# A delta net of chunk steps: the preparation, the doubling and the scan in one loop over the chunks

## What is computed

```python
decay = exp(where(incl, Gcum[..., :, None] - Gcum[..., None, :], -inf))
A = where(strict, einsum('bhnid,bhnjd->bhnij', k * beta, k) * decay, 0.0)
t_inv = triangular_solve(A + eye, eye, lower=True, unit_diagonal=True)
W = t_inv @ (k * beta * exp(Gcum))
U = t_inv @ (v * beta)
attn = einsum('bhnid,bhnjd->bhnij', q, k) * decay
def step(S, xs):
    v_new = U_n - W_n @ S
    o = q_n * exp(Gcum) @ S + attn_n @ v_new
    S = S * exp(G_total) + k_tail_n.T @ v_new
```

## Time and profile before

| what | value |
| --- | --- |
| median of 3 runs | 2021.78 us (2018.9 to 2022.38) |
| profiled execution, its own time | 2022.69 us |
| its span in the trace | 2020.9 us |
| granted PE clock, mean | 0.961 of full |
| delta net, from the phase end before it to the first branch matmul | 267.1 to 517.7 us of the span |

### The profile page before, as it was taken

The page is one execution under the profiler, slowest core; times in us unless marked ns, Lnnn a source line. Parts: engine busy times, 40 slices in busy tenths (PEclk is TensorE's granted clock), DMA queues, the critical chain, the costliest instruction groups (busy, mean ns, idle before and its releaser), DMA issues.

```text
span 2020.9 us, 34275 instructions
## 1 busy us (share of the span) xinstructions
PE 1845.8 (91%) x11766; PEld 1644.9 (81%) x11766; DVE 1273.1 (63%) x2464; ACT 1014.5 (50%) x2022; POOL 154.1 (8%) x116
## 2 busy tenths in 40 slices
PE   7999978778789997689999999999999997989997
PEld 1877867778678997678899999999899886879997
DVE  1684347777425997966666666666676665236776
ACT  2445533333015667866655555555557655016655
POOL 0000003221015452000000000000000000000000
PEclk9899978889889999999999999999999998999999
DMA  7423202222234552035555555555454432444553
GB/s 266 174 102 105 84 11 94 81 81 70 90 108 167 177 177 73 1 104 194 195 183 187 186 187 186 187 187 187 156 178 148 157 116 92 137 145 157 183 181 124
DMA packets 77266, 283.72 MB, mean 140 GB/s; under 512 B 8576, under 2 KB 8576, under 8 KB 76800
## 3 DMA queue, kind: packets, MB, share of 16 engines
q1 hardware_dynamic: 77184, 282.62, 40.9%
HBM read 281.54 MB, written 1.05 MB: 140 GB/s over the span
## 4 chain that ended last, share of the span: by engine, by line
PE 69%; DVE 13%; ACT 3%; issue 1%; POOL 1%; POOLq 0%; DVEq 0%; ACTq 0%
PE banks L702 17%; PE banks L690 16%; PE banks L764 8%; PE banks L897 6%; PE banks L654 6%; PE banks L909 3%; PE banks L575 2%; DVE split L1791 2%; PE banks L589 1%; PE banks L869 1%; DVE arena L1789 1%; DVE arena L1629 1%; DVE arena L1592 1%; PE banks L778 1%; PE banks L641 1%
## 5 line engine op out<-in xcount | busy, mean ns | idle before, releaser
L1130 ACT ACTIVATE split<-arena 128x512 fp32r<-128x512 f32 x508 | 319.1, 629 | 146.7 <-PE banks L690 83.2
L690 PEld LDWEIGHTS banks<-split 128*128 128x128 f32 x3072 | 379.5, 192 | 12.8 <-POOL split L2146 3.4
L690 PE MATMUL banks<-split 128*128 128x256 f32 x3072 | 383.0, 283 | 4.8 <-POOL split L2146 2.3
L702 PE MATMUL banks<-split 128*128 128x512 f32 x1536 | 365.0, 392 | 2.7 <-issue 2.7
L1805 DVE TENSOR_TENSOR split<-arena,split 128x512 fp32r<-128x512 f32 x412 | 281.6, 690 | 117.0 <-ACT split L1130 111.3
L702 PEld LDWEIGHTS banks<-split 128*128 128x128 f32 x1536 | 284.5, 189 | 58.8 <-issue 2.9
L1120 ACT ACTIVATE split<-arena 128x512 fp32r<-128x512 f32 x264 | 163.6, 626 | 73.2 <-PE banks L764 29.8
L764 PE MATMUL banks<-split 128*128 128x256 f32 x1344 | 169.3, 286 | 4.0 <-DVE split L1887 3.9
L764 PEld LDWEIGHTS banks<-split 128*128 128x128 f32 x1344 | 164.6, 193 | 7.6 <-issue 5.9
L424 PE MATMUL banks<-split 128*128 128x256 f32 (+2 forms) x936 | 152.3, 325 | 8.2 <-DVE split L1451 7.2
L424 PEld LDWEIGHTS banks<-split 128*128 128x128 f32 (+1 forms) x936 | 135.6, 198 | 26.9 <-issue 8.8
(11 more groups left out here) (365 smaller groups left out, 2398.9 us busy)
## 6 DMA issues: line engine op xcount, KB each, us to landing
arena<-wstream SPq DMA_DIRECT2D x525, 512.0 KB, 3.2
arena<-x_t SPq DMA_DIRECT2D x1, 2048.0 KB, 12.3
arena<-matsa SPq DMA_DIRECT2D x1, 1234.0 KB, 6.4
arena<-mats SPq DMA_DIRECT2D x1, 1024.0 KB, 9.3
out_t<-arena SPq DMA_DIRECT2D x4, 256.0 KB, 2.1
arena<-crow SPq DMA_DIRECT2D x1, 512.0 KB, 7.2
arena<-rows SPq DMA_DIRECT2D x1, 512.0 KB, 3.9
arena<-mats SPq DMA_DIRECT2D x1, 449.0 KB, 3.9
```

What stands on the lines that cost most here:

```text
L690: mm = pe.matmul(ps[:, 4 + b, 0:S], w_parts[:, c, (2 * m + half) % 4, P * k:P * k + P], h_parts[:, e, 4 * half + k, :], start=(half == 0 a ...
L702: mm = pe.matmul(ps[:, 2 * tt + half, :], g_parts[:, e, j % 2, P * tt:P * tt + P], w_parts[:, c, (2 * m + half) % 4, :], start=(first and ...
L1130: act.activation(w_parts[:, 0, (2 * m + half) % 4, :], ring[:, peer_slot(m), 512 * half:512 * half + 512], ACT.Copy).then_inc(sem["w_hi"], 1)
```

## The change

The three pieces become one loop of four steps.

- The small decay functions move into the attention phase; sigmoid is made from an exponential and a reciprocal, and a dummy exponential loads the table before the stage. One phase end is dropped.
- Within a level, PE multiplies the unmasked A with only those 64 columns a head of Z that the level changes (`parts`), VectorE masks the product (`packed`, 128x256) while it takes it out of PSUM, and the update has 64 columns too. ScalarE moves only the turned Z. Level 1 also turns Z, since T isn't made apart any more. Six of the seven masks and GpSimd's mask products go.
- While step n goes through its levels, the next chunk is prepared at fixed levels: rows of decays at 1, gaps and key products at 2, decayed keys, betas and the first mask on VectorE (`decayed_keys`, `mask_keys`) at 3, query products at 4, the turn of the mask at 5, the first Z at 6. Key products are now made for each direction apart, since the backward direction takes its own chunk order (`scan`).
- The scan of step n - 1 runs inside step n, and tokens are turned in levels 1 to 4 of step 0. GpSimd scales keys, values and states instead of masking.
- One tail stands at each level's end instead of one behind each Z, two in four of the levels; four more stand ahead of the loop. Silu and sigmoids of gates move to step 3.
- In the attention phase half of the attention output is turned earlier, and spread roots use three banks.

The core of the diff: PE's levels and loop, VectorE's helpers and loop, GpSimd's loop.

```diff
+            def level_products(n, l, d):
+                z, a = pair[d][f"Z{n % 2}"], pair[d][f"A{n % 2}"]
+                if l == 1:
+                    pe.wait_ge(sem["z1_ready"], step_at(n, d))
+                else:
+                    pe.wait_ge(sem["z_ready"], level_at(n, l - 1, d))
+                for h in range(4):
+                    mm = pe.matmul(ps[:, d, 64 * h:64 * h + 64], a[:, h, :], parts(z[:, h, :], l, 1 - d), start=True, stop=True)
+                mm.then_inc(sem["y_done"], 1)
...
+                    mm = pe.transpose(ps[:, 2 + d, P * h:P * h + P], z[:, h, :], ident)
+                mm.then_inc(sem["z_turned"], 1)
+
+            def level_update(n, l, d):
+                if l < 6:
+                    pe.wait_ge(sem["y_out"], 10 * n + 2 * (l - 1) + d + 1)
+                else:
+                    pe.wait_ge(sem["y_last"], step_at(n, d))
+                pe.wait_ge(sem["t_ready"], level_at(n, l, d))
+                r = slice(0, P) if l < 6 else slice(64 * d, 64 * d + 64)
+                for h in range(4):
+                    mm = pe.matmul(ps[:, d, 256 + 64 * h:320 + 64 * h], pair[d]["T"][r, h, :], yp[d][r, 64 * h:64 * h + 64],
+                                   start=True, stop=True)
+                mm.then_inc(sem["p_done"], 1)
+
...
+            for n in range(4):
+                for l in range(1, 7):
+                    for d in range(2):
+                        level_products(n, l, d)
+                    if n == 0 and l < 5:
+                        tok_turn(2 * l - 2)
+                        tok_turn(2 * l - 1)
+                    for d in range(2):
+                        if n and l == 1:
+                            state_write(0, d) if n == 1 else state_read(n - 1, d)
+                        if n == 3 and l == 2:
+                            query_read(2, d)
+                        if n >= 2 and l == 3:
+                            state_write(n - 1, d)
+                        if n == 3 and l == 4:
+                            out_write(2, d)
+                        if n == 3 and l == 5:
+                            query_read(3, d)
+                        if 1 <= n < 3 and l == 4:
+                            query_products(n + 1, d)
+                    for d in range(2):
+                        level_update(n, l, d)
+                    if n < 3:
+                        for d in range(2):
+                            if l == 1:
+                                decay_rows(n + 1, d)
+                            if l == 2:
+                                key_products(n + 1, d)
+                            if l == 5:
+                                mask_turn(n + 1, d)
                 for d in range(2):
-                    pe.wait_ge(sem["gb_ready"], 2 * n + d + 1)
-                    for h in range(4):
...
+            def gap_rows(n, d):
+                dve.wait_ge(sem["g_rows"], step_at(n, d))
+                e = pair[d]["E"]
+                gap = e if n < 2 else at[:, 2 * d + scan[d][n], :, :]
+                link(dve.tensor_tensor(gap, bank(4 + d, 4, P), head("G", n, d), ALU.subtract))
+                o = dve.tensor_scalar(e, gap, 0.0, None, ALU.max)
+                if n >= 2:
+                    link(o)
+                    o = dve.tensor_scalar(gap, gap, 0.0, None, ALU.min)
+                o.then_inc(sem["gaps"], 1)
+
+            def decayed_keys(n, d):
+                dve.wait_ge(sem["decays"], step_at(n, d))
+                dve.wait_ge(sem["k_products"], step_at(n, d))
+                dve.tensor_tensor(pair[d][f"A{n % 2}"], pair[d]["E"], bank(4 + d if n else 6 + d, 4, P), ALU.mult).then_inc(sem["a_raw"], 1)
+
+            def mask_keys(n, d):
+                b = pair[d]
+                a = b[f"A{n % 2}"]
+                dve.wait_ge(sem["a_raw"], step_at(n, d))
+                link(dve.tensor_tensor(a, a, head("beta", n, d), ALU.mult))
+                dve.tensor_tensor(b["E"], a, bc(level[:, d, :], 1, 4), ALU.mult).then_inc(sem["mask_ready"], 1)
+
+            def decayed_queries(n, d):
+                s = at[:, 2 * d + scan[d][n], :, :]
+                dve.wait_ge(sem["q_products"], step_at(n - 2, d))
+                dve.tensor_tensor(s, s, bank(4 + d, 4, P), ALU.mult).then_inc(sem["at_raw"], 1)
+
+            def first_inverse(n, d):
+                dve.wait_ge(sem["m_turned"], step_at(n, d))
+                dve.tensor_tensor(pair[d][f"Z{n % 2}"], bc(ident, 1, 4), bank(4 + d, 4, P), ALU.subtract).then_inc(sem["z1_ready"], 1)
+
...
+            for n in range(4):
                 for l in range(1, 7):
                     for d in range(2):
...
+                            dve.wait_ge(sem["y_done"], level_at(n, l, d))
+                            dve.tensor_tensor(yp[d].rearrange("p (a b) -> p a b", a=4), ps[:, d, 0:256].rearrange("p (a b) -> p a b", a=4),
+                                              bc(packed[:, d, l - 1, :], 1, 4), ALU.mult).then_inc(sem["y_out"], 1)
+                        elif n < 3:
+                            first_inverse(n + 1, d)
+                    for d in range(2):
+                        dve.wait_ge(sem["p_done"], level_at(n, l, d))
+                        z = parts(pair[d][f"Z{n % 2}"].rearrange("p a b -> p (a b)"), l, 1 - d)
+                        dve.tensor_tensor(z, z, ps[:, d, 256:512].rearrange("p (g s) -> p g s", s=2 ** l), ALU.subtract).then_inc(sem["z_ready"], 1)
+                    for d in range(2):
+                        if n == 1 and l == 1:
+                            new_state(0, d)
+                        if n >= 2 and l == 1:
+                            new_values(n - 1, d)
+                        if n == 3 and l == 2:
+                            query_scale(2, d)
+                        if n < 3 and l == 2:
+                            gap_rows(n + 1, d)
+                        if n < 3 and l == 3:
+                            decayed_keys(n + 1, d)
+                        if n >= 2 and l == 3:
+                            new_state(n - 1, d)
+                        if 1 <= n < 3 and l == 4:
+                            decayed_queries(n + 1, d)
+                        if n == 3 and l == 4:
+                            out_add(2, d)
+                        if n == 3 and l == 5:
+                            query_scale(3, d)
+                    for d in range(2):
+                        if n < 3 and l == 3:
+                            mask_keys(n + 1, d)
+                    for q in range(2 if (n, l) in ((0, 1), (0, 2), (3, 4), (3, 5)) else 1):
+                        mod_tail(next(tails))
+
...
-                for l in range(1, 6):
+                for d in range(2):
+                    if n >= 2:
+                        scale_state(n - 1, d)
+                for d in range(2):
+                    scale_tokens(n, d)
+                if n < 3:
                     for d in range(2):
-                        b = pair[d]
-                        pool.wait_ge(sem["y_done"], 14 * n + 2 * l + d + 1)
-                        pool.tensor_tensor(b["M"], b["A"], bc(level[:, d, l + 1, :], 1, 4), ALU.mult).then_inc(
-                            sem["late_mask"], 1)
-            phase_end(pool, 3)
+                        tail_tokens(n, d)
+                    if n:
+                        for d in range(2):
+                            mask_queries(n + 1, d)
```

More of the change, by code:

```diff
@@ L1047, in _ @@
                         act.activation(l2q[:, c, :], src, ACT.Square).then_inc(sem["l2_squares"], 1)
+                if g == 3:
+                    act.activation(small[:, 84:85], eps, ACT.Exp)
+                    output_moved(0)
                 in_out(a + 3)
-            for qt in range(2):
-                act.wait_ge(sem["o_turned"], qt + 1)
-                act.activation(oaT[:, :, P * qt:P * qt + P], bank(3 + qt, 4, P), ACT.Copy).then_inc(sem["o_moved"], 1)
+            output_moved(1)
@@ new lines, in _ @@
+                        act.wait_ge(sem["z_turned"], level_at(n, l, d))
+                        act.activation(pair[d]["T"].rearrange("p a b -> p (a b)"), ps[:, 2 + d, :], ACT.Copy).then_inc(
+                            sem["t_ready"], 1)
+                    if n == 0 and l < 5:
+                        tok_move(2 * l - 2)
+                        tok_move(2 * l - 1)
+                    for d in range(2):
+                        if n < 3 and l == 3:
+                            decays(n + 1, d)
+                        if n < 2 and l == 5:
+                            rows_of(n + 2, d, dec["G"][:, scan[d][n + 2], 4 * d:4 * d + 4])
@@ L1102, in _ @@
+            for i, tt in enumerate((1, 0)):
+                act.wait_ge(sem["head_stat"], i + 1)
+                act.activation(small[:, 72 + 4 * tt:76 + 4 * tt], small[:, 72 + 4 * tt:76 + 4 * tt], ACT.Sqrt, bias=eps, scale=1.0 / P).then_inc(
+                    sem["head_root"], 1)
+            phase_end(act, 2)
             for k in range(KT):
@@ new lines, in _ @@
```

(18 more changed lines are left out.)

551 lines of the change are left out of this document (278 added, 273 removed).

## The result

The changed kernel takes 2000.93 us (median of six runs, 1995.22 to 2006.62), the kernel before beside it 2021.20 us (2018.78 to 2022.38): ratio 0.9902, 95% interval 0.9875 to 0.9928. It is faster by 20 us; the forecast was 41 us. The time lies inside the forecast range, 20 us above the forecast, and on the figure of its second rival.

A forecast was written before the change was run, and what follows sets the result against it. TensorE, busy 91% of the span, was taken as the bound. 2022.7 - 14.7 (preparation, net of attention) + 0.6 (loop) - 27.7 (tail) = 1980.9, stated as 1981 us; range 1956 to 2003.

The forecast's parts named there:

- rival 2: Loop: clock falls at both stalls in every step and stays down; six drops of 4 or 5 us, 2001; chance 0.16.
- I count three drops, 7.5 us: Chunk loop: TensorE falls to half clock three times, at about 2.5 us each as at chunk starts before.
- 42 to 48: Expected sign in the profile after: chunk steps of 42 to 48 us.
- the prediction's own signs of being wrong: Levels well under 4.4 us, loop clock share far from 0.9, or stages after 549 us changing.
- Rival 3: Slower than before: a third of the loop at half clock eats the 41.8 us gain, half gives 2025 or more; chance 0.06.
- The halving is worth nothing to PE: Loop levels: 64-column matmuls take 0.11 us a record, just as 128-column ones, so a level stays at 4.66 us.
- Levels: Chunk loop: PE's own pace of 4.66 us a level for 40 records; 24 levels give 111.8 us.
- Stalls: Loop waits at level 2, between levels 3 and 4, at level 5, and for GpSimd (4 us); sum 21.8 us.
- Preparation: From attention phase's end to first level product: VectorE's operations in a row take 10.3 us, against 25.6.
- Attention: Attention phase: extra table load and activation +1.5 us, earlier output turning saves some 0.9; net +0.6.
- Tail: After the last inverse: remaining scan and head norm take 11 us against 38.7, a gain of 27.7.
- After: Stages after the delta net keep their instructions, and their weights still arrive in time: no change.

The follow-up runs named there:

- again: The changed kernel run once more with nothing changed; 2004.03 us (1984.41 to 2006.35, six runs).
- fill: The changed kernel plus 42 matmuls nobody reads, in TensorE's waits ahead of level 4's first update and the next chunk's key products; 1975.9 us.
- order0: The changed kernel with decay rows ahead of the first key products on TensorE in the preparation; 1998.02 us.
- narrow: The changed kernel with level products and updates moving 32 columns a head instead of 64, inverse not formed; 2017.98 us, one run.
- wide: The changed kernel with products taking all 128 columns of Z and updates moving their 64 columns twice; 1980.38 us.
- wide_fill: The changed kernel with 128 columns in level products and updates, plus unread matmuls in TensorE's waits at key products and level 4; 1972.24 us.
- first profile: The profiled execution among the changed kernel's first six runs, nothing altered; 1996.71 us.
- best: smooth plus unread matmuls: 5 ahead of the key products, 2 ahead of level 4's updates; 1971.31 us.
- smooth: The changed kernel with 128 columns, direction 1's betas and mask at level 4, tails moved to level 6, later logarithm, decay rows before key products; 1969.76 us.

## Why the prediction missed by 20 us

The loops of the profiled executions, in microseconds (half: time at half clock; idle: of TensorE):

| kernel | columns | loop | half | idle |
|---|---|---|---|---|
| before | 128 | 186.4 | 42.6 | 31.3 |
| changed | 64 | 198.4 | 69.9 | 12.6 |
| again | 64 | 191.9 | 53.2 | 13.9 |
| fill | 64 | 176.5 | 14.1 | 5.6 |
| order0 | 64 | 207.0 | 88.7 | 12.6 |
| narrow | 32 | 222.3 | 128.1 | 11.3 |
| wide | 128 | 180.3 | 16.2 | 15.2 |
| wide_fill | 128 | 175.7 | 4.1 | 6.8 |

**The step that failed is the clock: "I count three drops, 7.5 us".** There were six, and with the 0.39 us that the loop pays for each microsecond at half clock the clock cost 21 to 27 us. That is rival 2, in place, number (six; five in **again**) and price (4 or 5 us each: 64.9 x 0.39 / 6 = 4.2); it had a chance of 0.16 and named 2001.

The price of 2.5 us was not far off for the kernel before. Of the 42.6 us at half clock in its loop TensorE was idle in 15.6; the rest held 114 records, each some 0.1 us longer than at full clock, which is 11 us for three chunk starts and the end of a fourth drop. What was wrong is to carry this price over to work of half the columns, and to take shorter idle times for a relief. With 128 moved columns they are one (**wide**: 16.2 us at half clock against 42.6 before); with 64 each of the six drops the clock in the first profile, and it stays down over the work behind it, 10.8 us on average. The steps show the same: 50.2, 50.6 and 58.6 us where 42 to 48 were forecast, and 39.1 for the last step, which has no such wait and no time at half clock: 355 records at 0.11. The loop's clock share of 0.82 is one of the prediction's own signs of being wrong.

Rival 3 had a third of the loop at half clock eat the whole gain. Measured, 35% of the loop's time lay there, but only 331 of its 1378 records, a quarter; rival 3 needed a third of the records.

That the median falls on rival 2's figure is in part luck. In the profiled execution, 1996.7 us, the clock's 20 us beyond the 7.5 are met by waits 9 us shorter than forecast, and the attention phase and the preparation add 8. It is luck, too, that **wide** ran at 1980.38 us, which is the forecast: its loop is 7 us below the forecast's 187, its attention phase and preparation some 6 above.

The Trainium skill, "TensorE: Matmul & The Clock Gate", section "Terms", puts the penalty at the throttled time times the missing share of the clock, here 0.5 us for each microsecond. By that rule I estimate 35 us of clock in the changed loop, not 27. The pairs of runs above give 0.38 to 0.46. A record at half clock takes 0.204 us instead of 0.108, which would be 0.47; where the rest goes is not shown, since TensorE is idle in only 1.5 of the 69.9 us.

**Halved columns.** "The halving is worth nothing to PE" holds for the pace: 16 records in 1.71, 1.73 and 1.79 us with 32, 64 and 128 columns. It does not hold for the clock, where the halving costs: **wide** gets 12 to 18 us of the loop back. I had no such term. The rule by which levels would shorten (the Trainium skill, same page, section "Back-to-back issue gap") is not borne out here, where every matmul brings its own weights: 0.107 us a record with 32 columns, 0.112 with 128. The Trainium skill's rule on loads by columns (same page, section "LDWEIGHTS (loading the stationary operand)") is: by it I estimate some 107 ns for 128 columns.

**Levels** run a little faster than the 4.66 us taken: in **fill**, updates of two levels stand 317.05 - 312.59 = 4.46 us apart. In the sum this does not show: 198.4 less 27 for the clock and 12.6 of waits leaves 158.5 us for the forecast's 157.6. **Stalls**: PE idles 12.6 us in the loop, forecast 21.8 with GpSimd's share. The tails of 128x1024 take 1.37 us on average in the loop against 1.22 alone, so few meet GpSimd. In one line: forecast 187 = 165 busy + 22 idle, measured 198.4 = 185.8 + 12.6.

**Preparation**: forecast 10.3, measured 12.66. VectorE's list was right, but I let TensorE be ready. In its order 16 key products (3.34 us, mostly at the half clock) stand ahead of the decay rows for which VectorE waits. Timeline of the changed kernel:

```profile
274.94 3.34 PE L560 MATMUL banks<-arena 128*128 128x128 f32 x16
...
278.11 1.04 PE L552 MATMUL banks<-arena 128*128 128x128 f32 x8
278.82 0.69 DVE L1699 TENSOR_TENSOR arena<-banks,arena 128x512 f32<-128x512 f32 x1 [2.48 <-PE banks L552]
```

**order0** shows it: 10.90 with the two exchanged. **Attention**: forecast +0.6, profiled +6.5, in **again** +0.5. The wait for ScalarE grew from the 1.19 of the earlier trace rows to 2.73, the 1.5 us that I had put there; the rest goes with the clock (36.9 us at half clock against 22.7 in **again**) and differs between executions. **Tail**: forecast 11, measured 11.31, and 11.4 in nearly all kernels. **After**: forecast no change, measured -4.3 in the profiled execution, which spends 7.7 us less at half clock there (51.7 against 59.4); other kernels here show 1499 us with 52 at half clock, or 1502 to 1503 with 58 to 62, for the same instructions. What picks between the two is open.

So the sum by its own terms, for the profiled executions: 2022.7 + 6.5 - 12.9 + 12.0 - 27.3 - 4.3 = 1996.7.

## What to carry to other kernels

Take the price of TensorE's lower clock from the records that lie in it over the whole stretch, not from the stretch's mean clock alone (before, TensorE was idle in a third of that time), and look at what the matmuls around a gap move: idle times of 1.4 to 2.6 us went with 16 us at half clock beside 128-column work, and 53 to 89 beside 64-column work (**again**, the first profile, **order0**). Where matmuls load their own weights, narrowing the moved operand saves TensorE nothing and may cost clock; pack the columns only if another engine needs it, as here VectorE. Unread matmuls in a wait are a cheap test of whether the clock is the cause, and work that is moved away from a wait can make the next one, as here where it landed beside GpSimd's.

## What was not expected of the hardware

- Fewer moved columns at the same record rate mean more time at the lower clock: 128 us of a 222 us loop with 32 columns (one run, other numbers), 53 to 89 of 192 to 207 with 64, 16 of 180 with 128, with nearly the same waits (11 to 15 us). With 32 it fell twice with no wait at all.
- TensorE can be busy throughout and stay down: 10.24 us and 23.89 us at a granted clock of 0.50.
- The same program varies by 22 us (1984.41 to 2006.62 over twelve runs) in step with its mean clock, 0.965 to 0.952, while **wide** and **best** stay within 3 us (**smooth** does not: 11).
- 42 matmuls that nobody reads shorten the kernel by 25 to 28 us.
